# Eight TensorE products into an unread bank, in the last expert batch of each layer

## What is computed

```python
def hier_moe(h, lw):
    ...                                       # gate: top group, top 2 experts in it
    a = jnp.einsum("nd,edf->nef", t, lw["moe_w1"])
    b = jnp.einsum("nd,edf->nef", t, lw["moe_w3"])
    y = jnp.einsum("nef,efd->nd", jax.nn.silu(a) * b * gate[..., None], lw["moe_w2"])

x = x + g2 * hier_moe(modulate(rms_norm(x, lw["norm2_g"]), sh2, sc2), lw)
```

## Time and profile before

| | |
|---|---|
| median of 3 runs | 1218.31 us (1216.5 to 1219.31) |
| the profiled execution | 1220.88 us |
| span in it, first to last instruction | 1218.6 us |
| mean granted TensorE clock | 0.958 of full speed |
| PE busy | 1107.6 us, 91% |
| DVE busy | 553.9 us, 45% |
| DMA, mean | 274 GB/s |

### The profile page before, as it was taken

One profiled execution on the slowest core, in us unless ns is written; L12 is line 12 of the kernel. 1 busy time (PEld: TensorE's weight loads), 2 busy tenths in 40 slices (PEclk: granted clock), 3 DMA queues, 4 the chain that ended last, 5 costly groups with the idle time before them and its releaser, 6 DMA issues.

```text
span 1218.6 us, 18741 instructions
## 1 busy us (share of the span) xinstructions
PE 1107.6 (91%) x7521; PEld 545.0 (45%) x7521; DVE 553.9 (45%) x1414; ACT 292.9 (24%) x717; POOL 110.2 (9%) x126
## 2 busy tenths in 40 slices
PE   4899999898999998997789999979999999899775
PEld 1455554475566332332245655446755733233221
DVE  1246788366457211211162678936734742111124
ACT  0346522433222100010022672232331310010000
POOL 0011012410001000000101000331000100000001
PEclk9899999899998999999789999988999899999988
DMA  8572532866955999999954103385596399999995
GB/s 358 206 231 103 207 95 93 222 228 227 411 222 194 416 425 425 426 426 425 420 216 131 51 28 96 119 199 197 198 361 271 140 403 424 426 425 424 427 424 223
DMA packets 90794, 333.31 MB, mean 274 GB/s; under 512 B 29631, under 2 KB 32071, under 8 KB 59975
## 3 DMA queue, kind: packets, MB, share of 16 engines
q1 hardware_dynamic: 79911, 291.28, 61.0%
q0 software_dynamic: 7392, 23.93, 5.8%
q10 hardware_dynamic: 3392, 16.78, 3.4%
HBM read 314.40 MB, written 17.56 MB: 272 GB/s over the span
## 4 chain that ended last, share of the span: by engine, by line
PE 71%; DMA 12%; SPq 6%; DVE 5%; issue 3%; ACT 2%; DVEq 0%; ACTq 0%
PE bank L596 66%; DMA ring<-in_moe_w_dram 9%; SPq L1343 6%; PE bank L599 5%; DMA ring<-in_w_in_dram 2%; ACT arena L1516 2%; DVE small L2194 1%; DVE x L1876 1%; DVE ring L1876 1%; DVE arena L1868 1%; DVE x L1868 1%; DVE bank L1868 1%; DVE small L1876 0%; SPq L1397 0%; SPq L1432 0%
## 5 line engine op out<-in xcount | busy, mean ns | idle before, releaser
L596 PE MATMUL bank<-ring,arena 128*32 128x512 f32 (+1 forms) x2256 | 381.8, 587 | 8.7 <-DMA ring<-in_moe_w_dram 3.9
L596 PE MATMUL bank<-arena 128*32 128x512 f32 (+3 forms) x1616 | 315.1, 572 | 35.9 <-DMA ring<-in_moe_w_dram 13.5
L596 PE MATMUL bank<-ring,hT 128*128 128x512 f32 x576 | 257.9, 602 | 4.8 <-DMA ring<-in_w_in_dram 3.8
L1516 ACT ACTIVATE arena<-bank 128x512 f32<-128x512 f32 (+3 forms) x292 | 124.9, 468 | 567.7 <-PE bank L599 385.9
L596 PEld LDWEIGHTS bank<-ring,arena 128*32 128x32 f32 (+1 forms) x2256 | 108.4, 114 | 145.4 <-issue 145.1
L596 PEld LDWEIGHTS bank<-ring,hT 128*128 128x128 f32 x576 | 109.0, 194 | 131.0 <-issue 126.8
L596 PEld LDWEIGHTS bank<-arena 128*32 128x32 f32 (+2 forms) x1616 | 91.9, 124 | 164.3 <-issue 146.5
L596 PE MATMUL bank<-hT,ring 128*128 128x384 f32 x384 | 128.2, 488 | 0.0
L1868 DVE TENSOR_TENSOR arena<-bank,mrow 128x512 f32<-128x512 f32 x36 | 24.9, 692 | 223.5 <-PE bank L596 223.5
L596 PEld LDWEIGHTS bank<-hT,ring 128*128 128x128 f32 x384 | 71.2, 190 | 46.6 <-issue 1.3
L599 PE MATMUL bank<-const,arena 128*128 128x128 f32 x443 | 66.2, 283 | 18.5 <-DMA x<-in_x_prompt_dram 8.6
(11 more groups left out here) (163 smaller groups left out, 857.5 us busy)
## 6 DMA issues: line engine op xcount, KB each, us to landing
ring<-in_moe_w_dram SPq DMA_DIRECT2D x120, 1024.0 KB, 24.0
arena<-in_moe_w_dram SPq DMA_DIRECT2D x72, 1024.0 KB, 26.7
ring<-in_ada_w_dram SPq DMA_DIRECT2D x20, 2048.0 KB, 8.7
ring<-in_w_in_dram SPq DMA_DIRECT2D x14, 2048.0 KB, 10.3
ring<-in_ada_w_dram ACTq DMA_DIRECT2D x4, 2048.0 KB, 9.9
ring<-in_w_out_dram SPq DMA_DIRECT2D x4, 2048.0 KB, 9.0
expert_dram<-arena ACTq DMA_DIRECT2D x16, 512.0 KB, 8.4
tok_dram<-arena POOLq DMA_DIRECT2D x6, 512.0 KB, 3.8
```

The costliest lines, as they stand in the source:

```text
L596: return nc.tensor.matmul(out, lhsT, rhs, start=start, stop=stop)
L1516: return nc.scalar.activation(out, in_, func, **kw)
```

## The change

`last_phases` gets a helper, `kept_busy`, that issues products with the identity as the stationary operand and 512 columns of constants as the moving one, into `bank[0]`. Four stand ahead of b, two ahead of the transposes, two ahead of y: eight for each layer. They wait for nothing and set no semaphore. Nothing else is changed.

```diff
+                    def kept_busy(times):
+
+                        for _ in range(times):
+                            mm(bank[0][:], ident, const[:, 0:512])
+
                     def last_phases():
+                        kept_busy(4)
                         second_product(end - 1)
+                        kept_busy(2)
                         h_cols(end - 1)
+                        kept_busy(2)
                         results(end - 1)
                         direct(direct_full)
```

## The result

The changed kernel is slower: 1231.2 us (median of 4 runs, 1226.1 to 1232.8) against 1218.8 us, a ratio of 1.0097 with a 95% interval of 1.0062 to 1.0131. The direction was forecast; +4.4 us was not enough, and the median lies above the range. On two other chips, beside the kernel before on each, the same kernel came to 1.0076 (1.0042 to 1.0111) and 1.0063 (1.0039 to 1.0086). So the change costs about 8 to 12 us (0.0063 x 1213 to 0.0097 x 1219).

The account below looks back on a forecast made before the run. The prediction took PE's work in each layer's last expert batch as the bound, with the gap ahead of b being the branch. It summed +6.86 + 0.2 + 1.3 - 4.0 = +4.4 us to 1222.7 us, range 1218.8 to 1226.5.

Parts of the forecast that it names:

- Step 1: Four products ahead of b, behind the branch: nothing covers them, full-clock cost 3.43 us a layer, +6.86 us in all.
- Step 2: Two products ahead of the transposes: they just fit PE's wait after b; +0.2 us for both layers, ends -1.2 to +0.7.
- Step 3: Two products ahead of y: partly covered by ACT's copy, y starts 0.65 us late; +1.3 us for both layers.
- Step 4: Clock stays up through y once PE has no gap: 1.4 and 2.6 us back, together -4.0 us, or -2.8.
- The lag: DVE's start 0.57 and 1.56 us after b's last record: PE's own time, or a delay added products may remove.
- Rival A: Products run in the gap ahead of b, if the branch ends before 1179.6: about -8 us, 1210 us; chance 0.05.
- Step 5: What is late next: last weight piece lands at about 1196, y starts at about 1199 and doesn't meet it.
- Rival B: Lag vanishes and clock gives back 2.6 us in each layer: +1.3 us, 1219.6 us, not measurably slower; chance 0.13.
- Rival C: Products of constants do not bring the clock up: about +11 us a layer, 1240 us; chance 0.07.

Follow-up runs that it names:

- two_h: Against the kernel before: only the two products between phase b and the transposes added, chip 9; ratio 0.9995 (0.9976 to 1.0015).
- two_y: Against the kernel before: only the two products between the transposes and phase y added, chip 9; ratio 1.0005 (0.9980 to 1.0030).
- four_b: Against the kernel before: only the four products ahead of phase b added, inside the branch, chip 9; ratio 1.0038 (1.0012 to 1.0065).
- four_b_c: Only the four products ahead of phase b added to the kernel before, on chip 4; ratio 1.0038 (1.0014 to 1.0061).
- ahead_b: Against the kernel before: only four products a layer, ahead of the count's load and the branch, chip 7; ratio 1.0025 (1.0009 to 1.0041).
- before_3: The kernel before, unchanged, profiled on chip 7 beside the changed kernel, which measured 1.0076 against it.
- ahead_b_two_h: Against the kernel before: four products ahead of the branch and two between b and the transposes, chip 7; ratio 0.9985 (0.9963 to 1.0006).
- before_e: The kernel before, unchanged, run once more on chip 3 for its trace; no time of its own is given.
- after_c: The changed kernel with all eight products, run again on chip 4; ratio to the kernel before 1.0063 (1.0039 to 1.0086).
- after_late: The changed kernel, with POOL also waiting for the transposes before its gathers, chip 9; ratio 1.0051 (1.0029 to 1.0073).
- hoist_after: The changed kernel with its eight products, last phases moved ahead of the count's load and branch, chip 3; ratio 0.9982 (0.9949 to 1.0015).
- hoist: The kernel before with the last phases moved ahead of the count's load and branch, no products, chip 3; ratio 0.9999 (0.9972 to 1.0026).

## Why the prediction was right and wrong

**Step 1 held.** The gap is the branch, the products stand behind it and nothing covers them. *a* is 9.58 us in the mean of the ten places without the four (the three profiles of before, two_h, two_y) and 12.83 us in the sixteen with them in the branch: 3.25 us a layer, forecast 3.43. The mean bears out what was worked out there, that the slow clock doesn't make the four dearer; single places scatter by 1.6 us, as the clock rose earlier or later.

**Step 2 was mis-sized.** Without a lag the two products make *c* 0.50 us longer (10.04 for 9.54; 10.99 for 10.50), forecast 0.1. The cover was taken from the layer where it had been stretched by the lag; in an ordinary execution it is 0.5 us shorter. The upper end took as much off the cover, for another reason (the lag as PE's own time), and had 0.35.

**Step 3 was mis-sized.** The last two cost 0.96 us (10.50 for 9.54), forecast 0.65.

**Step 4 failed.** It took 1.4 and 2.6 us back from the clock, from one execution in which it had fallen in both layers. In the kernels without products between b and y (the three profiles of before, four_b, four_b_c, ahead_b) it fell at 6 of 12 places, and cost 1.7 to 3.0 us where it did: 13.4 us in twelve places, 1.1 us a layer, so -2.2 us where -4.0 was put in. That the products keep the clock up agrees with the 18 places that have them, of which 1 fell; what failed is the size, taken from one draw in which both places fell. This is the largest error, and the prediction had the warning in hand: it wrote that the moment may differ from run to run, and let the range end at 1.4 us a layer, never at none.

With the measured sizes the sum is 2 x (3.25 + 0.50 + 0.96 - 1.11) = **+7.2 us**. (The changed kernel itself lost 1.66 us to the clock at one of its six places; charged at the mean, that makes +7.8.) Measured on chip 4, where no lag was seen, 0.0063 x 1213 = +7.6 us (4.7 to 10.4).

**The lag.** In the two measurements in which the changed kernel shows it (the first, and chip 7), it is 2.35 to 2.75 us there and 0.12 to 1.56 us in the kernel before, in the mean 2.6 against 0.9 us, and it hides the two products of step 2: 1.7 - 0.5 = 1.2 us a layer, which would make +9.6 us of the +7.2. Measured: +11.8 us (7.6 to 16.0) in the first, +9.2 (5.1 to 13.5) on chip 7. For the change as a part of the cause: on chip 7, at the six places of before_3, ahead_b and ahead_b_two_h it is 1.34 us at most, and at both places of the changed kernel above 2.3. Against it: before_e has 2.85 us without any product, and after_c 0.12 us with all eight. Four_b and after_late never ran on a chip that has the lag, so whether the change makes it longer there is open. The prediction's two readings of it (PE's own time, or a signal that added products may hasten) are both wrong: it isn't PE's time, since in the changed kernel the two products stand at once behind b and are done before DVE starts (1193.59 to 1195.57, then 1196.41 above), and products behind b don't take it away. What holds back the signal of b's last product stays open.

**Rival A** is settled: the branch ended at 1181.3, not before 1179.6, and the products ran behind it. With the branch out of the way (hoist_after) the change isn't slower. But the rival's price, -8 us, is not borne out: hoist shows -3.4 to +3.2 us. It was worked out from one execution whose y ended 9.5 and 6.8 us behind the last weight piece; in the other four places of the kernel before it was 3.8 to 10.1 us, with a floor of 3.8. Step 5 held for the change: the last piece landed at 1196.6, as forecast, and y ended 8.6 us or more behind the last piece in all six places of the changed kernel.

**Rival B** needed more than 3 us a layer back from the clock, and no lag. At the six places of the kernel before the clock took 2.96 us at most and nothing at three. **Rival C** is out: under the four products of constants the clock rose at 1184 to 1186.

The Trainium skill, TensorE: Matmul & The Clock Gate, Loop structure matters more than you think, has it that a long wait between matmuls lets PE go cold. Its example waits for a DMA. The rows here agree in part: of the twelve places, the clock fell at 4 of the 5 where the lag, and with it the wait of PE, was 0.57 us or more, and at 2 of the 7 where it was 0.12 us or less. So a longer wait made a fall likelier, and decided no single place.

That the branch is long because of a fetch (the Trainium skill, Runtime: NRT & Kernel Launch, Instruction fetch mechanics) can be read from the DMA records of the instruction queue. In the thirty branches of the kernels with the branch ahead of b, a fetch of 16 KB starts 3.3 to 3.6 us behind the branch's start, and in 29 of them the branch ends 1.5 us behind the landing of the fetch. In the three hoist kernels the branch of the second layer stands where the weight stream has ended; there the fetch starts 1.0 us behind it, and the branch takes 3.3 to 3.6 us.

## What to carry to other kernels

Before filling a gap, look at what the engine's sequencer does in it: a gap that is a branch can't be filled by instructions behind the branch, they only queue ahead of the real work, at their full price. A clock loss read from one execution is one draw of several; size what you hope to win back by the mean over places and executions, and let the range end at none. Here the products did keep the clock up; what they saved was smaller than their price. And ask how far the phase stands from the next floor, in more than one execution: here the gap ahead of b fell from 3.65 to 1.24 us with no gain that could be measured, and y then ended 3.8 us behind the last weight piece at five of six places.

## What the runs showed of the hardware

- PE's compare-and-branch over one conditional block took 5.7 to 7.4 us in the kernels with the branch ahead of b (422 to 429 GB/s of DMA beside it in the first profile), and 3.3 to 3.6 us in the second layer of the hoist kernels, when the weight stream had ended (5 to 13 GB/s). A 16 KB fetch of the instruction queue landed 1.5 us before its end (1.4 us in the latter).
- The semaphore increment of a matmul can reach the waiting engine so late that DVE starts 2.85 us after the matmul's record ends (before_e), where 0.11 us is usual. It was seen in the first profiles and on chips 7 and 3, not on 9 and 4; the cause is open.
- The clock fell between b and y at 6 of 12 places without added products there, and at 1 of 18 with them.
- Four products issued ahead of a branch (8 matmul records) made it end 7.9 to 8.0 us behind the start of the y half before it, for 7.4 us in the mean without them.
